# One decoder step of two layers: where a side step stands between the two products of a SwiGLU tile

## The reference

```python
for layer in range(2):
    x = layer_norm(alpha*x + 0.5*swiglu(x, *ffn1[layer]))      # silu(x@w_gate) * (x@w_up) @ w_down
    if layer == 0:
        qa, ka, va, qb, kb, vb, gb = split(x @ w_in, 7)        # 512 columns each
        mix = concat(moba_attention(qa, ka, va), silu(gb)*group_norm(retention(qb, kb, vb))) @ w_out
    else:
        y = s5_scan(x)                                         # 64 groups x 64 complex states
        mix = (gelu(y) @ s5_w_out) * sigmoid(gelu(y) @ s5_w_gate)
    x = layer_norm(alpha*x + mix)
    x = layer_norm(alpha*x + 0.5*swiglu(x, *ffn2[layer]))
```

## Time and profile before

| | us |
|---|---|
| span of the profiled execution | 2521.5 |
| its whole time | 2523.19 |
| median of the runs | 2521.86 |
| PE, DVE, ACT, POOL busy | 2406.6, 1626.5, 1085.6, 462.6 |
| one `w_hi` of ACT (L257), mean | 1.035 |
| one `w_lo` of DVE (L266), mean | 1.283 |

### The profile page before, as it was taken

How to read it: one execution, slowest core, us unless ns; L and a number is a source line. 1 busy time by engine, 2 the same in 40 slices (tenths; PEclk the granted TensorE clock), 3 DMA queues, 4 the chain that set the end, 5 groups by cost and what they waited for, 6 DMA issues and landing times.

```text
span 2521.5 us, 46325 instructions
## 1 busy us (share of the span) xinstructions
PE 2406.6 (95%) x18811; PEld 2268.6 (90%) x18811; DVE 1626.5 (65%) x2536; ACT 1085.6 (43%) x1663; POOL 462.6 (18%) x532
## 2 busy tenths in 40 slices
PE   7999999999998999999999999999999899999998
PEld 6988998999788777789999999999999898999997
DVE  4787776666765555567686566466656485587555
ACT  3433355433553333453254534554433536354333
POOL 4886710002100011300111101021001010121000
PEclk8999999999999999999999999999999999999999
DMA  7657766435446687644566556555555566555553
GB/s 173 177 163 204 206 191 199 121 114 146 120 140 195 203 278 218 171 124 127 142 177 175 167 146 206 171 152 151 154 149 149 168 184 203 152 158 146 151 151 96
DMA packets 676277, 417.31 MB, mean 166 GB/s; under 512 B 31554, under 2 KB 639682, under 8 KB 676066
## 3 DMA queue, kind: packets, MB, share of 16 engines
q1 hardware_dynamic: 669538, 393.98, 54.2%
q0 software_dynamic: 6528, 20.37, 2.7%
HBM read 395.51 MB, written 18.78 MB: 164 GB/s over the span
## 4 chain that ended last, share of the span: by engine, by line
PE 77%; DVE 12%; ACT 4%; issue 3%; DMA 2%; SPq 1%; POOL 0%; ACTq 0%; DVEq 0%; POOLq 0%
PE ps L271 21%; PE ps L272 20%; PE ps L273 20%; DVE w_lo L266 4%; PE ps L908 2%; PE ps L910 2%; PE ps L909 2%; ACT w_hi L257 2%; PE ps L1620 1%; PE ps L2307 1%; PE ps L1669 1%; DMA w_raw<-in_ffn_w_up 1%; DVE x L558 1%; PE ps L1641 1%; DVE h_lo L460 1%
## 5 line engine op out<-in xcount | busy, mean ns | idle before, releaser
L266 DVE TENSOR_TENSOR w_lo<-w_raw,w_hi 128x1024 fp32r<-128x1024 f32 (+1 forms) x648 | 828.3, 1283 | 607.8 <-ACT w_hi L257 605.1
L271 PE MATMUL ps<-x_hi,w_hi 128*128 128x256 f32 (+1 forms) x3200 | 973.0, 304 | 38.5 <-DVE w_lo L266 29.4
L272 PE MATMUL ps<-x_lo,w_hi 128*128 128x256 f32 (+1 forms) x3200 | 957.6, 299 | 0.0
L273 PE MATMUL ps<-x_hi,w_lo 128*128 128x256 f32 (+1 forms) x3200 | 957.3, 299 | 0.0
L257 ACT ACTIVATE w_hi<-w_raw 128x1024 fp32r<-128x1024 f32 (+1 forms) x648 | 669.8, 1035 | 572.5 <-PE ps L273 412.1
L271 PEld LDWEIGHTS ps<-x_hi,w_hi 128*128 128x128 f32 x3200 | 617.8, 193 | 57.7 <-DVE w_lo L266 38.8
L272 PEld LDWEIGHTS ps<-x_lo,w_hi 128*128 128x128 f32 x3200 | 618.0, 193 | 1.2 <-issue 0.4
L273 PEld LDWEIGHTS ps<-x_hi,w_lo 128*128 128x128 f32 x3200 | 617.4, 193 | 0.0
L271 PE MATMUL ps<-h_hi,w_hi 128*128 128x256 f32 (+1 forms) x1408 | 423.0, 300 | 12.3 <-DVE w_lo L266 9.4
L273 PE MATMUL ps<-h_hi,w_lo 128*128 128x256 f32 (+1 forms) x1408 | 414.4, 294 | 0.0
L272 PE MATMUL ps<-h_lo,w_hi 128*128 128x256 f32 (+1 forms) x1408 | 414.4, 294 | 0.0
(11 more groups left out here) (263 smaller groups left out, 2193.0 us busy)
## 6 DMA issues: line engine op xcount, KB each, us to landing
w_raw<-in_ffn_w_gate SPq DMA_DIRECT2D x176, 512.0 KB, 4.3
w_raw<-in_ffn_w_up SPq DMA_DIRECT2D x176, 512.0 KB, 3.9
w_raw<-in_ffn_w_down SPq DMA_DIRECT2D x128, 512.0 KB, 4.0
w_raw<-in_w_in_ab SPq DMA_DIRECT2D x56, 512.0 KB, 4.1
w_raw<-in_ffn_w_down SPq DMA_DIRECT2D x64, 384.0 KB, 3.6
arena<-in_cache_k SPq DMA_DIRECT2D x64, 256.0 KB, 4.5
arena<-in_cache_v POOLq DMA_DIRECT2D x64, 256.0 KB, 5.0
w_raw<-in_w_out_ab SPq DMA_DIRECT2D x16, 512.0 KB, 3.9
```

The source lines that it names most:

```text
L266: dve.tensor_tensor(T.w_lo[:, u % RING, 0:n], T.w_raw[:, u % RAW, 0:n], T.w_hi[:, u % RING, 0:n].bitcast(F32), ALU.subtract).then_inc(T.w_ ...
L271: pe.matmul(out, w_hi, m_hi, start=first, stop=False)
L272: pe.matmul(out, w_hi, m_lo, start=False, stop=False)
L273: return pe.matmul(out, w_lo, m_hi, start=False, stop=last)
```

## The change

`fine` has three values: none, `EARLY` and `LATE`. `LATE` is what `fine` was. `EARLY` differs on ACT and DVE: in a tile the first side step comes ahead of tanh and the second rounding on ACT, and ahead of the second rest and silu on DVE. PE, POOL and SP do not tell the two apart. `f3a[:2]` gets `EARLY` on all engines, `f2a[:1]` gets `LATE` where it had none, `f1a` keeps `LATE`. No instruction, wait or DMA is added or taken away.

```diff
+EARLY, LATE = 1, 2
@@ ffn_scalar
         round_piece(T, act, u + LEAD)
         if d is None:
+            if fine == EARLY:
+                yield
             act.wait_ge(T.w_used.h, u + 1)
             act.activation(T.gate[:, i % 2, 0:g.n], T.ps[:, T.banks[o], 0:g.n], ACT.Tanh, scale=0.5)\
                .then_inc(T.tanh_done.h, 1)
             round_piece(T, act, u + 1 + LEAD)
-            if fine:
+            if fine == LATE:
                 yield
@@ tensor (scalar, vector, gpsimd and sync alike)
-            weave(ffn(ffn_tensor, pe, f2a[:1]), after(split.tensor(pe), after(ret_b.tensor(pe), ret_s.tensor(pe))))
+            weave(ffn(ffn_tensor, pe, f2a[:1], LATE), after(split.tensor(pe), after(ret_b.tensor(pe), ret_s.tensor(pe))))
...
-            weave(ffn(ffn_tensor, pe, f3a[:2], True), beside_b(N3B.tensor(pe), s5_b.tensor(pe)))
+            weave(ffn(ffn_tensor, pe, f3a[:2], EARLY), beside_b(N3B.tensor(pe), s5_b.tensor(pe)))
```

More of the change, by code:

```diff
@@ L2804, in layers, with ffn @@
         block = ctx.enter_context(nc.Block())
-        def ffn(of, eng, parts, fine=False):
+        def ffn(of, eng, parts, fine=None):
             for part in parts:
@@ L2850, in _ @@
             run(project_sync(T, sp, PB1))
-            weave(ffn(ffn_sync, sp, f1a, True), after(after(idle(2 * att_b.STEPS - 3), samples.begin(sp)), samples.sync(sp)))
+            weave(ffn(ffn_sync, sp, f1a, LATE), after(after(idle(2 * att_b.STEPS - 3), samples.begin(sp)), samples.sync(sp)))
             ret_s.load(sp, I["state_ret"][0], ((T.sa_valued, BP),))
             run(project_sync(T, sp, PB2))
-            run(ffn(ffn_sync, sp, f2a[:1]))
+            run(ffn(ffn_sync, sp, f2a[:1], LATE))
             run(out_sync(T, sp, OB))
@@ L2860, in _ @@
             run(ffn(ffn_sync, sp, f2b))
-            weave(ffn(ffn_sync, sp, f3a[:2], True), beside_b(idle(Norm.STEPS), s5_b.sync(sp, O)))
+            weave(ffn(ffn_sync, sp, f3a[:2], EARLY), beside_b(idle(Norm.STEPS), s5_b.sync(sp, O)))
             run(out_sync(T, sp, OB2))
@@ L2880, in _ @@
             weave(project_tensor(T, pe, PB1), N1A.tensor(pe))
-            weave(ffn(ffn_tensor, pe, f1a, True), after(after(idle(1), spaced(att_b.tensor(pe))), samples.tensor(pe)))
+            weave(ffn(ffn_tensor, pe, f1a, LATE), after(after(idle(1), spaced(att_b.tensor(pe))), samples.tensor(pe)))
             weave(project_tensor(T, pe, PB2), N2A.tensor(pe))
-            weave(ffn(ffn_tensor, pe, f2a[:1]), after(split.tensor(pe), after(ret_b.tensor(pe), ret_s.tensor(pe))))
+            weave(ffn(ffn_tensor, pe, f2a[:1], LATE), after(split.tensor(pe), after(ret_b.tensor(pe), ret_s.tensor(pe))))
             run(out_tensor(T, pe, OB))
@@ L2903, in _ @@
             weave(project_scalar(T, act, PB1), N1A.scalar(act))
-            weave(ffn(ffn_scalar, act, f1a, True), after(after(idle(1), spaced(att_b.scalar(act))), samples.scalar(act)))
+            weave(ffn(ffn_scalar, act, f1a, LATE), after(after(idle(1), spaced(att_b.scalar(act))), samples.scalar(act)))
             weave(project_scalar(T, act, PB2), N2A.scalar(act))
-            weave(ffn(ffn_scalar, act, f2a[:1]), after(split.scalar(act), after(ret_b.scalar(act), ret_s.scalar(act))))
+            weave(ffn(ffn_scalar, act, f2a[:1], LATE), after(split.scalar(act), after(ret_b.scalar(act), ret_s.scalar(act))))
             run(out_scalar(T, act, OB))
@@ L2911, in _ @@
             weave(ffn(ffn_scalar, act, f2b), N4A.scalar(act))
-            weave(ffn(ffn_scalar, act, f3a[:2], True), beside_b(N3B.scalar(act), s5_b.scalar(act)))
+            weave(ffn(ffn_scalar, act, f3a[:2], EARLY), beside_b(N3B.scalar(act), s5_b.scalar(act)))
             run(out_scalar(T, act, OB2))
@@ L2930, in _ @@
             weave(project_vector(T, dve, PB1), N1A.vector(dve))
-            weave(ffn(ffn_vector, dve, f1a, True), after(after(idle(1), spaced(att_b.vector(dve))), samples.vector(dve)))
+            weave(ffn(ffn_vector, dve, f1a, LATE), after(after(idle(1), spaced(att_b.vector(dve))), samples.vector(dve)))
             weave(project_vector(T, dve, PB2), N2A.vector(dve))
-            weave(ffn(ffn_vector, dve, f2a[:1]), after(split.vector(dve), after(ret_b.vector(dve), ret_s.vector(dve))))
+            weave(ffn(ffn_vector, dve, f2a[:1], LATE), after(split.vector(dve), after(ret_b.vector(dve), ret_s.vector(dve))))
             run(out_vector(T, dve, OB))
@@ L2938, in _ @@
             weave(ffn(ffn_vector, dve, f2b), N4A.vector(dve))
-            weave(ffn(ffn_vector, dve, f3a[:2], True), beside_b(N3B.vector(dve), s5_b.vector(dve)))
+            weave(ffn(ffn_vector, dve, f3a[:2], EARLY), beside_b(N3B.vector(dve), s5_b.vector(dve)))
             run(out_vector(T, dve, OB2))
@@ L2958, in _ @@
             weave(project_gpsimd(T, pool, PB1, O), N1A.gpsimd(pool))
-            weave(ffn(ffn_gpsimd, pool, f1a, True), after(idle(2 * att_b.STEPS + 1), samples.gpsimd(pool)))
+            weave(ffn(ffn_gpsimd, pool, f1a, LATE), after(idle(2 * att_b.STEPS + 1), samples.gpsimd(pool)))
             ret_s.clear_blocks(pool, ((T.sa_valued, BP), (T.acc_added, N2A.added + KT - 1)))
             weave(project_gpsimd(T, pool, PB2, O), N2A.gpsimd(pool))
-            weave(ffn(ffn_gpsimd, pool, f2a[:1]),
+            weave(ffn(ffn_gpsimd, pool, f2a[:1], LATE),
                   after(idle(1 + 4 * len(ret_b.tiles)), ret_s.gpsimd(pool, O["state_prompt"], O["state_sample"])))
@@ L2968, in _ @@
             weave(ffn(ffn_gpsimd, pool, f2b), N4A.gpsimd(pool))
-            weave(ffn(ffn_gpsimd, pool, f3a[:2], True), beside_b(N3B.gpsimd(pool), s5_b.gpsimd(pool)))
+            weave(ffn(ffn_gpsimd, pool, f3a[:2], EARLY), beside_b(N3B.gpsimd(pool), s5_b.gpsimd(pool)))
             run(out_gpsimd(T, pool, OB2))
```

## The result

| | before | after |
|---|---|---|
| median of 6 runs each, us | 2521.91 (2520.21 to 2528.7) | 2510.03 (2508.35 to 2514.01) |
| profiled execution, whole time | 2523.19 | 2509.77 |

The ratio is 0.9949, 95% interval 0.9939 to 0.9959: faster by 11.9 us, where 9.6 was forecast (2512.5, range 2508 to 2520).

What follows compares the result with a forecast made beforehand. TensorE, busy 95% of the span, bounds the kernel. Retention 3.5 plus norm 4.0 and scan 2.1 make 9.6 us off 2523.2: 2513.6 profiled, 2512.3 on the median's scale, stated as 2512.5, range 2508 to 2520.

Steps and rivals of the forecast that it cites:

- Part 1: Retention stage: 24 side-step slots in place of 16 remove 10.8 us and add waits and lowered clock; net 3.5 us gained.
- turn 1: Retention, first token tile: TensorE newly waits about 0.4 us for DVE's chain of 7.0 us.
- turn 2: Retention, second token tile: TensorE newly waits about 1.2 to 1.5 us for DVE's chain of 7.85 us.
- step 14: Retention, sample state updates in the last tiles: a new TensorE wait of 1.7 us, as DVE has more work.
- the 1.7 for a lowered clock on top: Retention: if the new waits come close together, the clock falls once for 3.4 us, costing 1.7 us.
- Part 2, the norm: Second norm beside S5: earlier centring and scaling on DVE end TensorE's wait for ACT's copies sooner; 4.0 us gained.
- Part 2, the scan: Scan beside the second S5: DVE's limiting chain ends 2.9 us earlier, of which 2.1 us is left as gain.
- the first down product takes 1.2 longer: Behind the scan: tanh and rounding follow GELU's load, GELUs and copies, so the last tile's h comes late; 1.2 us lost.
- The clock holds everywhere: Rival: both stages reach their good ends without lowered clock, 14.1 us gained, 2508 us; chance 0.15.
- The retention pays back: Rival: compressing DVE's work puts new waits together, so the retention gains zero; 2516 us, chance 0.17.
- the early step moves nothing: Rival: silu's later time holds TensorE, only the retention's gain is left, 2518.5; chance 0.16, shared with both halves shrinking.
- Slower: Rival: in the scan, up products wait for banks that silu frees later, 12 us in all; 2530 us, chance 0.07.

Runs made afterwards that it cites:

- kernel 1: The change with f3a[:2] put back to LATE, so only the retention's finer side steps remain; 2519.09 us, ratio 0.9987 to the kernel before.
- kernel 5: The change with the retention's 20 side steps spread over all 24 slots, one empty slot behind four of them; 2507.33 us, ratio 0.9938 to before.
- kernel 2: The change without LATE on f2a[:1], so only the early side step beside the second S5 remains; 2515.5 us, ratio 0.9967 to before.
- the repeats: The unaltered change and its version with the spread retention, each run once more on one chip; 2510.87 and 2505.8 us.
- kernel 3: The change with ACT back to tanh and second rounding ahead of the side step, early on DVE alone; 2509.41 us, ratio 0.9942 to before.
- kernel 7: The change with both the spread retention and the early step on DVE alone; 2507.63 us, ratio 0.9936 to before.
- the change again: The changed kernel run once more, unaltered, on another chip's measure of before; 2510.87 us, ratio 0.9955 to before.

## Why the prediction was right, and where it was not

**Part 1, 3.5 forecast, 4.2 measured.** What is removed held: no lowered clock at 1207 to 1218, OB starts 105.6 us behind the stage's start for 108.2 and runs at full pace (28.15 us for 29.71). The new waits step by step, forecast and measured: turn 1 0.4 and 0.44; turn 2 1.2 to 1.5 and 1.32; the samples' blocks 0.4 and 0.64; step 14 1.7 and 1.54; first down product 2.2 and 1.6 (kernel 1; in the change it is the lowered clock). That is 5.5 us for the 5.6 I took. The mis-sized term is the 1.7 for a lowered clock on top: in kernel 1 the clock does not fall (mean PEclk 1.00 over the whole stage) and in the change its fall swallows the last wait.

```profile
1104.90:1239.00 134.10, 128.56 (x1041) 124.44 (x1040) 99.11 (x173) 47.72 (x56) 12.14 (x16) 1.00 0.49 135
```

Without that term the sum is 10.8 less 5.5, 5.3, and the stage gained 4.2. Kernel 5 shows where the 1.1 us is: it has no lowered clock in the stage and 0.91 us of waits, so the stage's work is 127.6 us. Against this the kernel before lost 10.4 (137.93), 6.2 of them waits, so its lowered clock cost 4.2, where the prediction has 4.7 (with the 6.2 that is 10.9, which it writes as 10.8). Kernel 1 loses 6.2 (133.76), 5.5 of them waits and 0.7 in PE's busy time. Where these 0.7 come from no run shows.

**Part 2, the norm, 4.0 forecast, 5.65 measured** (5.5 to 6.2 in kernels 2 and 5 and the repeats). The steps held: centring 2.1 sooner forecast, 2.2 measured; reciprocal 2.9, 3.0; PE's wait for POOL 2.6, 2.55. The mis-sized term is the 1.7 of clock that I left out because three stalls remained. Over the whole part PE idles 5.78 us for 9.95, 4.2 less, which is the 4.0; and it is busy 67.45 us for 68.93, 1.5 less, since the clock is lowered for 6.8 us (1962.1, window above) where it was for 10.2 (1954.9, and this window of before):

```profile
1978.80:1982.20 3.40, 3.40 (x19) 3.40 (x18) 2.15 (x3) 1.84 (x4) 0.00 (x0) 0.50 0.38 94
```

It now falls at g4, which took 5.49 us and ended when ACT's copies were there: the 2.4 us wait that I forecast for the copies is gone from the list. In kernel 2, kernel 3 and kernel 5 that wait is 0.46, 1.50 and 0.48. The slow products cost nothing there. The change's repeat has 3.4 us of lowered clock in this part in place of 6.8 and takes the same time (73.12 for 73.23), with PE idle for 1.3 us more. Kernels 3 and 7 above are the opposite case: there DVE itself waits for the slowed product, and 3.4 us of lowered clock cost 1.5.

**Part 2, the scan, 2.1 forecast, 3.3 measured, and 1.8 in kernels 2, 3, 5 and the change again.** DVE's chain came 3.0 nearer, 2.9 forecast: `fixed_d` stood 53.8 us behind the part's start (the row of before follows, the part started at 2039.75), now at 50.8 (its row below at 2080.41, the part starts at 2029.58).

```profile
2093.54 0.06 DVE L2488 MEMSET arena<- 128x1 f32 x1
```

PE goes on behind the stacked states 53.2 us behind the part's start for 56.1, in the change and in all kernels with the early step. The `w_lo` wait before g6 went from 4.58 to 1.84 us (1.9 forecast). The sum itself does not close: 2.9 less the 1.2 below is 1.7 and not 2.1, and the prediction does not show the other 0.4. The step that failed is "the first down product takes 1.2 longer". From the timelines of ACT, then DVE, behind the scan:

```profile
2083.61 1.28 ACT L2400 ACT_TABLE_LOAD   x1
2084.91 1.21 ACT L2400 ACTIVATE arena<-ps 40x512 f32<-40x512 f32 x2
...
2088.23 0.60 ACT L2353 ACTIVATE arena<-ps 128x512 f32<-128x512 f32 x1
2088.72 0.38 ACT L437 ACTIVATE gate<-ps 128x256 f32<-128x256 f32 x1
```

```profile
2080.41 0.06 DVE L2496 MEMSET arena<- 128x1 f32 x1
...
2091.36 0.41 DVE L456 SCALAR_TENSOR_TENSOR gate<-gate,ps 128x256 f32<-128x256 f32 x1
...
2092.59 0.42 DVE L468 TENSOR_TENSOR h_lo<-prod,h_hi 128x256 fp32r<-128x256 f32 x1
```

The four terms that the prediction lists ahead of tanh are as listed (1.28, 1.21, 2.06 and 0.60), but how they make 1.2 it does not show. There is no load between GELU and tanh. `h_lo` is there at 2093.01, and PE's eighth round of the first down product begins at 2093.64 by its timeline:

```profile
2091.10 0.36 PE L271 MATMUL ps<-h_hi,w_hi 128*128 128x256 f32 x1
...
2093.64 0.28 PE L271 MATMUL ps<-h_hi,w_hi 128*128 128x256 f32 x1
```

Nothing is lost: `h_lo` has 0.63 us to spare. What takes 1.5 back in kernels 2, 3, 5 and the repeat is the clock: around PE's wait for the stacked states (L2315; 2.0 us there, 1.3 in the change's first profile) it falls a second time. The length of that wait does not decide it: kernel 7 has the same 2.0 us, no second fall, and 61.93 us. Kernel 2, a narrow window and PE's first waits from 2033 on:

```profile
2087.80:2091.20 3.40, 3.40 (x26) 3.03 (x22) 1.04 (x1) 2.75 (x4) 0.00 (x0) 0.50 0.64 176
```

```profile
PE ps L271 <- DVE gate L456: 3.5, 2, 3.0
PE ps L2315 <- ACT arena L2353: 2.0, 1, 2.0
```

The waits for silu were forecast at 1.3 and 1.6 and are 0.54 and 2.98, the 3.5 in two of the list: 0.6 more together, and nearly all in one place. DVE is not idle there but busy with scan steps, so this is not the sign of being wrong that the prediction names.

**The rivals.** "The clock holds everywhere" asked 14.1: the profiled change has 13.2 in its stages, but lowered clock at three places, so its mechanism did not happen; two of the three stood where they cost little. "The retention pays back" and "the early step moves nothing" are refuted by the stages of kernels 1 and 2. "Slower" decides at `fixed_d`, which came sooner. Half of the edit was of no use: the prediction has the load and tanh behind Sqrt in the norm's chain, but it did not ask what the norm would be with ACT left alone, and kernel 3 shows that ACT's half costs some 2 us there.

**How sure.** The sum of 9.6 fell 2.3 short of the 11.9. The steps of the waits held to a few tenths, those of the clock did not: it came out better by 1.7 in part 1, by 1.5 in the norm and, in the first profile, by 1.5 in the scan, and the prediction had no rule for where it falls. That part is luck. The changed kernel's own repeat has 11.8 in its stages, the first profile 13.2: what differs between them is the scan's second lowered clock (61.5 for 63.0).

## What to carry to other kernels

An in-order engine that does a main loop and side work should do the side step first where it needs nothing from TensorE any more and others wait for it; where the step begins with a wait for TensorE, it must stand behind the loop's own work (140.3 us against 133.7). Before spacing side steps evenly, add up the other engine's chain between two of them: one product more at the four places where TensorE waited (in the turns 7 to 8 us of VectorE against 6.7 of TensorE) was worth more than the finer steps themselves (5.3 us against 4.2 in the stage). And price a lowered clock by what comes behind it: ahead of a wait that another engine ends it is free (133.70 us with it, 133.75 without), unless that engine itself waits for the slowed product (71.94 us with it, 70.44 without).

## What was not expected of the hardware

- ScalarE loads its tables between Sqrt and tanh (1.28 us), and not between GELU and a tanh that follows it (GELU at 2084.91, copies behind it, tanh at 2088.72). The trace of before shows it too: ScalarE's tanh at 1569.05, the first behind the GELUs of the first S5, has no load ahead of it.
- The same code has one lowered clock more or less from one execution to the next: the scan took 61.52 and 63.02 us in two profiles of the change.
